# Mixture-of-experts stage of a decoder trunk: two streams of weight units taken one by one in turn instead of two by two

## The reference, cut to what matters

```python
def swiglu(h, wg, wu, wd):
    return (jax.nn.silu(h @ wg) * (h @ wu)) @ wd

def moe_top2(h, router, wg, wu, wd):
    ...
    top_val, top_idx = lax.top_k(logits, TOP_K)
    gates = jax.nn.softmax(top_val, axis=-1)
    ...
    yb = lax.map(expert_block, (xb, block_exp))
    ys = yb.reshape(n_slots, d) * slot_gate[:, None].astype(h.dtype)
    y = jnp.zeros((t + 1, d), h.dtype).at[slot_tok].add(ys)[:t]
```

## Time and profile before

| | |
|---|---|
| Device time, median of 3 runs | 1451.28 us (1451.2 to 1451.77) |
| Device time of the profiled execution | 1451.71 us |
| Its span | 1449.9 us |
| TensorE busy, share of the span | 1385.0 us, 96% |
| VectorE busy | 864.9 us, 60% |
| ScalarE busy | 691.9 us, 48% |
| DMA, mean | 306 GB/s |
| Mean granted TensorE clock | 0.991 |

### The profile page before, as it was taken

How to read it: one execution, slowest core, us unless ns; L and a number is a source line. 1 busy time by engine, 2 the same in 40 slices (tenths; PEclk the granted TensorE clock), 3 DMA queues, 4 the chain that set the end, 5 groups by cost and what they waited for, 6 DMA issues and landing times.

```text
span 1449.9 us, 17407 instructions
## 1 busy us (share of the span) xinstructions
PE 1385.0 (96%) x6647; PEld 972.2 (67%) x6647; DVE 864.9 (60%) x966; ACT 691.9 (48%) x763; POOL 6.9 (0%) x14
## 2 busy tenths in 40 slices
PE   7999999999999999999999999999999999999987
PEld 6878888888797787655755555755555665656525
DVE  6996645553579968655545555455656455555425
ACT  6566543542555657444454534454444444443315
POOL 0000000000000000000000000000000000000000
PEclk9999999999999999999999999999999999999998
DMA  9415555555543019999999999999999999999991
GB/s 336 156 59 171 197 180 187 190 177 200 165 145 116 9 69 412 391 404 414 407 416 413 409 403 415 398 416 414 409 403 416 403 414 414 409 405 416 409 410 67
DMA packets 129618, 443.85 MB, mean 306 GB/s; under 512 B 6960, under 2 KB 21328, under 8 KB 114944
## 3 DMA queue, kind: packets, MB, share of 16 engines
q1 hardware_dynamic: 128640, 439.29, 78.4%
q0 software_dynamic: 896, 3.44, 0.6%
HBM read 440.61 MB, written 2.10 MB: 305 GB/s over the span
## 4 chain that ended last, share of the span: by engine, by line
PE 65%; DMA 17%; DVE 10%; ACT 4%; issue 4%; SPq 0%; DVEq 0%; ACTq 0%
PE psum L585 16%; PE psum L587 15%; PE psum L586 15%; PE psum L1086 10%; DMA ring<-in_moe_w_gate 9%; DMA ring<-in_moe_w_down 6%; DVE ring_lo L1924 4%; ACT w_hi L1430 3%; DMA ring<-in_moe_w_up 2%; PE psum L630 2%; PE psum L1014 1%; DVE arena_b L2405 1%; PE psum L648 1%; DVE arena_a L2005 1%; PE psum L608 1%
## 5 line engine op out<-in xcount | busy, mean ns | idle before, releaser
L1924 DVE TENSOR_TENSOR ring_lo<-ring,w_hi 128x2048 fp32r<-128x2048 f32 x169 | 386.9, 2291 | 334.2 <-ACT w_hi L1430 333.9
L1430 ACT ACTIVATE w_hi<-ring 128x2048 fp32r<-128x2048 f32 x169 | 323.1, 1912 | 382.3 <-DMA ring<-in_moe_w_gate 139.1
L1086 PE MATMUL psum<-ring,xT 128*64 128x512 f32 (+1 forms) x1472 | 307.6, 561 | 1.7 <-DMA ring<-in_moe_w_down 1.7
L1918 DVE TENSOR_TENSOR ring_lo<-ring,w_hi 128x2048 fp32r<-128x2048 f32 (+1 forms) x70 | 157.2, 2267 | 103.2 <-ACT w_hi L1424 103.2
L587 PE MATMUL psum<-w_hi,hidden_b 128*128 128x512 f32 x560 | 218.6, 390 | 0.0
L1086 PEld LDWEIGHTS psum<-ring,xT 128*64 128x64 f32 x1472 | 97.9, 136 | 166.8 <-issue 153.2
L585 PE MATMUL psum<-w_hi,hidden_b 128*128 128x512 f32 x448 | 181.9, 406 | 17.2 <-DVE ring_lo L1924 15.9
L586 PE MATMUL psum<-ring_lo,hidden_b 128*128 128x512 f32 x448 | 175.1, 391 | 0.0
L585 PE MATMUL psum<-w_hi,xT_parts 128*128 128x512 f32 (+1 forms) x384 | 150.5, 392 | 3.6 <-DVE xT_parts L1929 2.6
L587 PE MATMUL psum<-w_hi,xT_parts 128*128 128x512 f32 (+1 forms) x384 | 149.5, 389 | 0.0
L586 PE MATMUL psum<-ring_lo,xT_parts 128*128 128x512 f32 (+1 forms) x384 | 149.4, 389 | 0.0
(11 more groups left out here) (329 smaller groups left out, 1325.3 us busy)
## 6 DMA issues: line engine op xcount, KB each, us to landing
ring<-in_moe_w_gate SPq DMA_DIRECT2D x112, 1024.0 KB, 9.9
ring<-in_moe_w_up SPq DMA_DIRECT2D x112, 1024.0 KB, 10.0
ring<-in_moe_w_down SPq DMA_DIRECT2D x112, 1024.0 KB, 9.9
ring<-in_w_in SPq DMA_DIRECT2D x16, 1024.0 KB, 5.9
ring<-in_dense_w_gate SPq DMA_DIRECT2D x14, 1024.0 KB, 5.1
ring<-in_dense_w_up SPq DMA_DIRECT2D x14, 1024.0 KB, 5.1
ring<-in_dense_w_down SPq DMA_DIRECT2D x14, 1024.0 KB, 4.8
ring<-in_w_out SPq DMA_DIRECT2D x8, 1024.0 KB, 5.0
```

The costliest lines, as they stand in the source:

```text
L1086: last = mm(psum[half * LIGHT:half * LIGHT + LIGHT, b, 0:n], x, w[:, half * n:half * n + n], start=first, stop=final)
L1430: A(heavy_high(c), raw(g), ACT.Copy).then_inc(hi_ready, 1)
L1918: V.tensor_tensor(low(g, sizes[g]), raw(g, sizes[g]), f32(high(g, sizes[g])), ALU.subtract).then_inc(lo_ready, 1)
L1924: V.tensor_tensor(low(g), raw(g), f32(heavy_high(c)), ALU.subtract).then_inc(lo_ready, 1)
```

## The change

The two streams are taken one by one in turn: H0 L0 H1 L1 H2 L2 and so on, where it was H0 H1 L0 L1 H2 H3 L2 L3. It is one constant:

```diff
 PAIRS = NE // 2
 PAIR_UNITS = 2 * EXPERT_UNITS
-GROUP = 2
+GROUP = 1
```

## The result

The changed kernel takes 1620.79 us (median of 4 runs, 1618.36 to 1622.96) against 1451.53 us: ratio 1.1165, 95% interval 1.1151 to 1.118. The direction was forecast, the size not: 1568 us with 1538 to 1598 was given.

A forecast was written before the change was run, and what follows sets the result against it. The stream of weights was taken as the bound, TensorE close behind. Stalls 126.7 us plus switches 15.4, less 24.0 of TensorE's idle time and 1.7 for landed last weights, gave +116.4: 1568 us, range 1538 to 1598.

The forecast's parts named there:

- The bound: Expert stage before the change: the stream of weights sets the pace, 2.56 us a unit, with TensorE under 4% behind.
- the main term: Work tied to even light places waits for unfinished odd heavy units: twelve TensorE stalls, 35.5 us an iteration, 126.7 in all.
- The signs named for it: `ring_lo` waits about 35 us an iteration, iterations about 250 us, rates near 350 GB/s, landings sooner than 9.9 us.
- the part behind L28: End of an iteration, where no tied work waits for a later unit; it should keep its pace.
- its signs of being wrong: Iterations staying at 215 us, TensorE's waits being on landings, or a clock under 1.00 in the stage.
- rival D: The clock falls to half in TensorE's stalls, 2.5 us each: 1593 us (silus alone) to 1676; over 1598 given 6%.
- A smaller term: TensorE's heavy-light switches: 0.20 us a round trip, +4.2 us in each of iterations 1 to 3, 15.4 us in all.
- the silu at L10: Silu waiting for H11: chain ends 6.57 us after that heavy unit's end T, cover 2.45 us, so TensorE stalls 4.1 us.
- A: Rival: TensorE has more room than its matmul rows say and the stalls vanish in it; no change, 1452 us; chance 5%.
- B: Rival: the alternating weight stream is read faster, at 423 GB/s; -28 us, 1423 us; chance 3%.
- C: Rival: only half of the stalls bite, through earlier splits or the ring's lead; +40 to +85, about 1510 us; 7%.

The follow-up runs named there:

- the repaired alternation: Changed kernel with each piece of tied work moved one position later, to the heavy unit it waits for; 1453.01 us, ratio 1.0011.
- the kernel with filled stalls: Changed kernel with TensorE multiplying zeros during its stalls, in 256-column multiplies that end inside the stall; 1573.53 us, ratio 1.0846.
- a deeper lead: Changed kernel with splits four units ahead of TensorE in place of three; 1457.59 us, ratio 1.0043.
- hi parts first: Changed kernel with each heavy unit's eight hi-part matmuls before the wait for VectorE's rest, then the other four; 1504.21 us, ratio 1.0365.
- the two-by-two kernel: Kernel before, in its two-by-two order, with tied work at the odd heavy places, one position earlier than it had it; 1475.76 us, ratio 1.0171.

## Why the prediction came out wrong

**The bound and the main term held.** The stream set the pace before, TensorE stood 4% behind, and the tied work that waits for a unit one position on is the cause: twelve stalls of the lengths worked out (34.4 us from start to start, 35.5 forecast); the loss but for 0.1% goes when the places are moved. The signs named for it are there: TensorE's waits on `ring_lo`, the rates, the earlier landings, the part behind L28 without a stall. So is one of its signs of being wrong: the clock is under 1.00 in the stage, 0.95 in each of iterations 1 to 3.

**The step that failed is the clock, rival D.** The sum has no term for it: every unit is priced at full clock. The prediction held the fall for the unlikely case ("they are shorter, and heavy work fills the time between"), gave a time over 1598 a chance of 6%, and let the range end there. It went by one row, 4.75 us of idle before a clock of 0.50, and took shorter waits to be harmless. Its sentence that no row has a gap as long as the stalls is not right either: 4.75 us is longer than all of them. The trace had one of a stall's length too, though it was no clean case, since the clock had fallen before it began, in a stretch of broken work:

```profile
1411.00:1413.00 2.00, 1.57 (x7) 1.17 (x6) 2.00 (x3) 1.23 (x4) 0.00 (x0) 0.50 1.07 401
```
```profile
1415.21 0.77 PE L585 MATMUL psum<-w_hi,xT_parts 128*128 128x512 f32 x1 [2.64 <-DVE xT_parts L1929]
```

The runs show falls behind stalls of 1.74 to 3.97 us, behind seven of twelve in an iteration and 27 of 43 in all, at the price of 47.3 us, 1.75 each. D's price of 2.5 us a fall was somewhat high; what was missed is that falls come at all, and behind most stalls. The Trainium skill (TensorE: Matmul & The Clock Gate, The HAM clock gate) has idleness lower the clock; the rows agree, and show it for waits much shorter than the one in the trace before.

**A smaller term was mis-sized:** a round trip between heavy and light cost 0.37 us and not 0.20, since a heavy unit between two switches takes 2.98 us where the terms give 2.92, and a light one up to 1.90 and not 1.79: 7.8 us an iteration, not 4.2. It also leaves the repaired alternation 1.7 us an iteration over the stream. For all 77 more round trips that is 13 us too little in the sum. That the kernel with filled stalls lies only 5.5 us over the forecast is partly luck: the stalls were worked out some 4 us too long, and some 3 us more of other terms, which no run parts, go the same way. (In the working of the silu at L10 the parts add up to T + 6.51 and not T + 6.57; either gives the 4.1 us.)

**Rivals.** A falls: the stalls don't vanish in any room of TensorE's, as 34.4 us of them lengthen an iteration by 34.3. B stays open: even with the places repaired TensorE needs 216.8 us an iteration, so the stream, at 406 to 408 GB/s, could not show whether it can run faster than before. C falls: every stall that was listed is in the trace. What is not settled is which stall brings a fall and which not: in iteration 1 those at 815.51, 828.65, 896.92, 919.50 and 961.42 brought none, though one of them was of 3.37 us, and one that did was of 1.76. In iteration 2 it is partly other places.

## What to carry to other kernels

Where several engines follow one order written out by hand, a change of the order moves every wait relative to the work around it: list, for each engine, which unit a piece of work waits for and what that engine must still do before the waiting one can go on, and compare that chain with the cover. A stall on a TensorE that works nearly without pause can have a second price, the clock behind it, here from 1.74 us of idle on; put both in the range. Here no version beat the kernel before: the stream of weights bounded it, and the alternation can't take units faster than they land. The tied places, a deeper lead and hi parts first each took most of the loss back.

## What the runs showed of the hardware

The granted clock fell to 0.50 behind 27 of 43 waits of 1.5 to 4 us, though TensorE had worked without pause for 9.7 us and more before each, and came back within 3 to 7 us. Of the waits that brought a fall the shortest was of 1.74 us; 22 waits of 1.23 to 1.72 us in the two-by-two kernel brought none, and one of 3.37 us in the changed kernel none either. Filling the same stalls with multiplies of zeros kept it at full speed and made the kernel 47 us faster. A float32 multiply of 128 rows by 512 columns took about 0.8 us of TensorE and left two records in the trace (12 for six). So the 8 matmuls of a light unit, in the rows and in the description of the kernel before, are eight records of four float32 multiplies.
